# Leaving out the filler matmuls at the three sub-layer boundaries of a two-layer hybrid decoder trunk

## The chip, the cores and the metric

The kernel runs on one core of a Trainium2 chip. The metric is the time of one execution on the device, in microseconds (us); lower is better. A core has TensorE (matrix products, rows PE, with its weight loads PEld), VectorE (DVE), ScalarE (ACT), GpSimd (POOL) and SyncE (SP, which here only issues DMAs). Each engine runs its own instructions in order, and they meet through semaphores.

## The reference

One sequence of 256 tokens of width 1024 goes through two layers. Each layer is a token mixer and a channel mixer, and each of these four sub-layers stands between two root-mean-square norms:

```python
for l in range(DEPTH):                       # DEPTH = 2
    h = rms_norm(x, mix_pre_g[l]) * (1 + sc_m) + sh_m
    y = hybrid_mixer(h, w_in[l], ...)        # conv, stick-breaking attention, gated linear attention, w_o
    x = x + g_m * rms_norm(y, mix_post_g[l])
    h = rms_norm(x, ffn_pre_g[l]) * (1 + sc_f) + sh_f
    y = swiglu(...) if l % 2 == 0 else moe_swiglu(...)   # dense, then top 2 of 8 experts
    x = x + g_f * rms_norm(y, ffn_post_g[l])
```

`rms_norm` divides by the root of the mean square over the 1024 channels. So at a boundary between two sub-layers there is a sum over `y`, an update of `x`, and a second sum over the new `x`, each needed before the next step. The matmuls that the change concerns compute nothing of this.

## The kernel before

Activations lie with channels on the 128 partitions: `x`, `h` and `y` are 8 chunks of 128 channels by 256 tokens. Weights come as units of 1 MB (128 x 2048 floats) in one fixed order (`PLAN`, then the experts). For each unit SP loads `raw`, ACT rounds it to a high part (`write_hi`), DVE subtracts to make a low part (`write_lo`), and PE multiplies high by high, low by high and high by low (`parts`). A unit in `project` is 8 chunks of 6 matmuls of 256 columns.

Each engine's order is written out by hand in its own block. The dense layer and the mixers run unit after unit; the experts run in a loop. Between them lie three boundaries that take the same course: mixer to dense layer in layer 0, dense layer to mixer at the start of layer 1, and mixer to experts in layer 1. One boundary goes:

1. `norm_sums` on PE: matmuls of a matrix of ones (128 x 128) with the squares of `y` give in the bank `M` the sum over channels, on all partitions. This is full fp32, so one matmul leaves two records.
2. `keep_warm(u, 3)` on PE: three filler matmuls of the ones with a constant area of 512 columns, into a bank whose content has been read.
3. ACT `norm`: Ln and Exp give the reciprocal root. DVE `norm_out`: for each of 8 chunks one multiply and one add to `x`. ACT `norm_x` squares `x` two chunks at a time, and after each pair PE adds two matmuls (`norm_sums` again).
4. `keep_warm(u, 2)` on PE: two more fillers.
5. ACT `norm` again; DVE `norm_in` scales each chunk; ACT `shift` adds the bias and rounds; DVE makes the low part and signals `h_split`. PE's first unit (`project` with `ready`) takes up each chunk as it comes. At the third boundary the router's small matmuls come instead, chunk by chunk on `h_ready`.

`keep_warm` issues on PE alone; nothing waits for it and it signals no semaphore. It waits, through `wait_read`, until its bank has been read. No DMA is issued and no other engine's order is touched in it.

Of the kernel before, what the change touches and what calls it, by code (L numbers as in the profile page):

```python
# [30 lines left out]
P = 128  # L31
# [28 lines left out]
PAIRS = D_FF // 256  # L60
# [8 lines left out]
def z_columns():  # L69

    cols = [(CONV, False), (0, False), (CONV + 256, False), (256, False)]
    for part in range(3):
        cols += [(O_SB + 512 * part + 256 * h, part == 2) for h in range(2)]
    for part in range(4):
        cols += [(O_GLA + 512 * part + 256 * h, part == 2) for h in range(2)]
    cols += [(O_GATES + 256 * u, False) for u in range(G_UNITS)]
    return cols
# [98 lines left out]
C_ID, C_ONES, C_LNEG, C_NEG = (A_CONST + P * i for i in range(4))  # L176
# [9 lines left out]
def program(nc, x_t, vecs, c_row, glr_w, a2, router, stream, experts, out_t):  # L186
    with ExitStack() as ctx:
# [19 lines left out]
        bank = [ctx.enter_context(nc.psum_tensor(f"bank{i}", [P, 512], F32)) for i in range(8)]  # L207
# [5 lines left out]
        def area(at, *dims):  # L213
            n = int(np.prod(dims))
            v = ar[:, at:at + n]
            if len(dims) == 2:
                return v.rearrange("p (a b) -> p a b", a=dims[0])
            if len(dims) == 3:
                return v.rearrange("p (a b c) -> p a b c", a=dims[0], b=dims[1])
            return v  # L220
# [31 lines left out]
        ident, ones = area(C_ID, P), area(C_ONES, P)  # L252
# [120 lines left out]
        def mixer_units(layer):  # L373
            return [u for u in W_UNITS if u[1] == layer and u[0] in ("z", "out", "wo")]
# [4 lines left out]
        BANKS = {}  # L379
# [18 lines left out]
        def wait_read(eng, u):  # L398

            for b, before in BANKS[u]:  # L400
                eng.wait_ge(bank_read[b], before + 1)
# [464 lines left out]
        def _(dve):  # L866
# [257 lines left out]
            def moe_lo(step, k, rounds=0):  # L1124
                slot, _, s, w = moe_unit(step, k, rounds)
                dve.wait_ge(hi_written, w + 1)
                dve.tensor_tensor(expert_lo[s], raw[:, slot, :], f32(expert_hi[s]),  # L1127
                                  ALU.subtract).then_inc(raw_taken, 1)
# [210 lines left out]
        def _(pe):  # L1339
# [7 lines left out]
            def norm_sums(first=0, last=4, squares=squares, sums=M):  # L1347

                for q in range(first, last):
                    pe.wait_ge(norm_squares, 4 * norms[0] + q + 1)  # L1350
                    for c in (2 * q, 2 * q + 1):
                        mm = pe.matmul(sums[:, 0:T], ones, squares[:, c, :], start=(c == 0), stop=(c == KC - 1),  # L1352
                                       skip_group_check=True)
                if last == 4:
                    mm.then_inc(norm_sum, 1)
                    norms[0] += 1

            def keep_warm(u, count):

                wait_read(pe, u)  # L1360
                for _ in range(count):
                    pe.matmul(bank[BANKS[u][0][0]][:, :], ones, area(C_ID, 4 * P), start=True, stop=True)

            def begin(u):
                pe.wait_ge(raw_taken, POS[u] + 1)
                for b, before in BANKS[u]:
                    if before:
                        pe.wait_ge(bank_read[b], before)
                return SLOT[u]

            def project(u, hi, lo, ready=None, before=0, chunks=1):


                s = begin(u)
                out = two(bank[BANKS[u][0][0]])
                for k in range(KC):
                    if ready is not None:
                        pe.wait_ge(ready, before + k // chunks + 1)
                    for c in range(2):
                        for n, (w, high) in enumerate(parts(s)):  # L1380
                            mm = pe.matmul(out[:, c, :], w[:, 256 * k + P * c:256 * k + P * c + P],  # L1381
                                           (hi if high else lo)[:, k, :],
                                           start=(k == 0 and n == 0 and c == 0),
                                           stop=(k == KC - 1 and n == 2), skip_group_check=True)
                mm.then_inc(consumed, 1)
# [13 lines left out]
            def project_branch(u, hi, lo):  # L1399

                s = begin(u)
                for c in range(4):
                    out = two(bank[BANKS[u][c // 2][0]])
                    for k in range(4):
                        for n, (w, high) in enumerate(parts(s)):
                            mm = pe.matmul(out[:, c % 2, :], w[:, 512 * k + P * c:512 * k + P * c + P],
                                           (hi if high else lo)[:, k, :],
                                           start=(k == 0 and n == 0), stop=(k == 3 and n == 2))
                mm.then_inc(consumed, 1)
# [134 lines left out]
            def hook(layer, i):  # L1544
                if i == 0:
                    low_rank(layer)
                if 0 <= i - 12 < SB_HEADS:
                    stick_o(layer, i - 12)
                if 0 <= i - 11 < SB_HEADS:
                    stick_sum(layer, i - 11)  # L1550
                if 0 <= i - 10 < SB_HEADS:
                    if i == 10:
                        wait_read(pe, ("z", layer, 7, 0))
                    if i == 12:
                        wait_read(pe, ("z", layer, 9, 0))
                    stick_z(layer, i - 10)
                if i == 19:
                    log_a(layer, 0)
                if i == 20:
                    log_a(layer, 1)  # L1560
                if i == 23:
                    gla_turn(layer)
                if i == 24:
                    gla_states(layer)
                if i == 25:
                    gla_out(layer)
                if i == 26:
                    gla_sums(layer)
                    conv_sums(layer, conv_acc, conv_done, layer + 1, mean_ready)
                if i == 28:  # L1570
                    conv_sums(layer, conv_tmp, cv_squared, layer + 1, var_ready)

            norm_sums()
            for layer in range(DEPTH):
                if layer:
                    norm_sums(1, 4)
                    keep_warm(("gate", 0, PAIRS - 1, 0), 3)
                    norm_sums()
                    keep_warm(("gate", 0, PAIRS - 1, 0), 2)
                for i, u in enumerate(mixer_units(layer)):  # L1580
                    if i == 0:
                        project(u, h_hi, h_lo, h_split, 2 * layer * KC)
                    elif u[0] == "z":
                        (project_tokens if z_columns()[u[2]][1] else project)(u, h_hi, h_lo)
                    elif u[0] == "out":
                        b = u[2]
                        if b == 0:
                            pe.wait_ge(a_split, layer + 1)
                        if b == 2:
                            pe.wait_ge(c_split, layer + 1)  # L1590
                        if i == 32:
                            pe.wait_ge(cv_root, layer + 1)
                        project_branch(u, br_hi[b], br_lo[b])
                    elif u[2] == 0:
                        project(u, h_hi, h_lo, s_split, 4 * layer, 2)
                    else:
                        project(u, h_hi, h_lo)
                    hook(layer, i)
                    if i == 38:
                        norm_sums(0, 2)  # L1600
                norm_sums(2, 4)
                keep_warm(("wo", layer, 2, 0), 3)
                norm_sums()
                keep_warm(("wo", layer, 2, 0), 2)
                if layer == 0:
                    for i, u in enumerate(FFN_UNITS):
                        if u[0] == "down":
                            project_down(u)
                        elif i == 0:
                            project(u, h_hi, h_lo, h_split, KC)  # L1610
                        else:
                            project(u, h_hi, h_lo)
# [3 lines left out]
            for k in range(KC):  # L1616
                pe.wait_ge(h_ready, 3 * KC + k + 1)
                for t in range(2):
                    mm = pe.matmul(Z[0][:, 8 * t:8 * t + 8], hf[:, k, P * t:P * t + P], router_sb[:, k, :],  # L1619
                                   start=(k == 0 and t == 0), stop=(k == KC - 1), skip_group_check=True)  # L1620
# [226 lines left out]
```

## Time and profile before

| | us |
|---|---|
| median of 3 runs | 1854.64 |
| lowest to highest run | 1853.37 to 1854.91 |
| the profiled execution, its own time | 1851.58 |
| its span from first to last instruction | 1849.7 |
| PE busy in the span | 1782.7 |
| mean granted TensorE clock | 0.989 |

Times in rows are microseconds from the first instruction. The granted clock is the share of full speed that TensorE was given: 1.00 is 2.4 GHz, 0.50 is 1.2 GHz. A row of matmuls ends when the last result is out, so the row is longer than the time for which it keeps the next matmul waiting; the distance between two starts in a full queue tells that. "Idle before" in brackets is the time in which the engine stood still, and what released it.

### The profile page before, as it was taken

The page shows a single profiled execution, that of the slowest core. Times are in us where ns is not written, and L with a number is a line of the kernel's source. Part 1 is how long each engine was busy: PE and PEld are TensorE (multiplying, and loading weights), DVE is VectorE, ACT ScalarE, POOL GpSimd, SP SyncE. Part 2 cuts the span into 40 slices and gives each one's busy share as a digit, 9 for nine tenths or more (in the row PEclk, how much of TensorE's full clock was granted, in tenths as well). Part 3 has the DMA queues.
Part 4 walks back from the last instruction along what each step waited for, and adds up shares of the span by engine and source line. Part 5 has one row for each costly group of instructions (what it writes and reads, how often), then busy time and mean ns, then how long its engine had stood idle before and what let it go on. Part 6 is the DMA issues. An engine that isn't in the chain of part 4 may idle for free.

```text
span 1849.7 us, 28685 instructions
## 1 busy us (share of the span) xinstructions
PE 1782.7 (96%) x10843; PEld 1577.2 (85%) x10844; DVE 1533.6 (83%) x1422; ACT 1133.5 (61%) x954; POOL 193.6 (10%) x159
## 2 busy tenths in 40 slices
PE   2999999999999999989999999999999999999997
PEld 2999999899979999978888888888888888888886
DVE  6998866999657667767889898898898988988986
ACT  3444564533354554656777777767777777677774
POOL 0396001000006900000000000000000000000000
PEclk7999999999999999999999999999999999999999
DMA  9865534699735333444999989989999899899992
GB/s 381 356 239 200 175 138 163 229 392 362 260 108 185 135 137 137 160 153 181 364 355 363 373 330 375 366 338 363 353 361 372 330 376 370 335 366 348 361 374 94
DMA packets 72521, 525.30 MB, mean 284 GB/s; under 512 B 8112, under 2 KB 8240, under 8 KB 8704
## 3 DMA queue, kind: packets, MB, share of 16 engines
q1 hardware_dynamic: 72288, 524.03, 74.6%
q8 instruction: 54, 0.88, 0.2%
q0 software_dynamic: 160, 0.23, 0.0%
q14 instruction: 19, 0.16, 0.0%
HBM read 523.17 MB, written 1.05 MB: 283 GB/s over the span
## 4 chain that ended last, share of the span: by engine, by line
PE 55%; DVE 2%; ACT 0%; issue 0%; DVEq 0%; ACTq 0%
PE bank L1654 33%; PE bank L1669 16%; PE bank L1689 2%; PE bank L1679 1%; PE bank L1381 1%; PE bank L1352 1%; PE bank L1709 0%; PE bank L1710 0%; DVE arena L943 0%; DVE arena L947 0%; PE bank L1619 0%; DVE arena L1066 0%; PE bank L1626 0%; DVE w_lo L878 0%; DVE arena L1058 0%
## 5 line engine op out<-in xcount | busy, mean ns | idle before, releaser
L1127 DVE TENSOR_TENSOR w_lo<-raw,w_hi 128x2048 fp32r<-128x2048 f32 x224 | 510.0, 2291 | 82.9 <-ACT w_hi L752 82.9
L752 ACT ACTIVATE w_hi<-raw 128x2048 fp32r<-128x2048 f32 x224 | 428.5, 1916 | 97.0 <-PE bank L1669 70.4
L1381 PE MATMUL bank<-acts,w_hi 128*128 128x256 f32 x2080 | 374.2, 284 | 27.7 <-DVE acts L933 21.1
L1381 PEld LDWEIGHTS bank<-acts,w_hi 128*128 128x128 f32 x2080 | 321.4, 191 | 33.1 <-issue 24.6
L1654 PE MATMUL bank<-acts 128*128 128x512 f32 x1248 | 304.3, 392 | 2.5 <-DVE acts L1127 2.5
L1654 PE MATMUL bank<-w_hi,acts 128*128 128x512 f32 x960 | 297.3, 391 | 0.0
L1381 PE MATMUL bank<-acts,w_lo 128*128 128x256 f32 x1040 | 292.6, 281 | 0.0
L1654 PEld LDWEIGHTS bank<-acts 128*128 128x128 f32 x1248 | 231.3, 188 | 49.3 <-DVE acts L1127 2.9
L1127 DVE TENSOR_TENSOR acts<-raw,acts 128x2048 fp32r<-128x2048 f32 x112 | 256.1, 2287 | 19.9 <-ACT acts L752 19.9
L752 ACT ACTIVATE acts<-raw 128x2048 fp32r<-128x2048 f32 x112 | 215.1, 1921 | 72.2 <-PE bank L1654 69.8
L1669 PE MATMUL bank<-w_hi,acts 128*128 128x512 f32 x832 | 256.1, 389 | 0.0
L878 DVE TENSOR_TENSOR w_lo<-raw,w_hi 128x2048 fp32r<-128x2048 f32 x82 | 190.7, 2325 | 70.3 <-ACT w_hi L542 69.3
L542 ACT ACTIVATE w_hi<-raw 128x2048 fp32r<-128x2048 f32 x82 | 156.7, 1911 | 129.2 <-PE bank L1381 93.5
L1654 PEld LDWEIGHTS bank<-w_hi,acts 128*128 128x128 f32 x960 | 179.0, 188 | 36.3
L1381 PEld LDWEIGHTS bank<-acts,w_lo 128*128 128x128 f32 x1040 | 198.0, 190 | 0.0
L1654 PE MATMUL bank<-w_lo,acts 128*128 128x512 f32 x480 | 186.9, 389 | 0.0
L1669 PEld LDWEIGHTS bank<-w_hi,acts 128*128 128x128 f32 x832 | 156.2, 188 | 32.4
L1669 PE MATMUL bank<-w_lo,acts 128*128 128x512 f32 x416 | 161.9, 389 | 0.0
L891 DVE SCALAR_TENSOR_TENSOR raw<-raw,arena 128x1024 f32<-128x1024 f32 x96 | 116.7, 1252 | 13.1 <-DMA raw<-in_stream 12.1
L1654 PEld LDWEIGHTS bank<-w_lo,acts 128*128 128x128 f32 x480 | 90.1, 188 | 19.0
L489 POOL TENSOR_SCALAR arena<-arena 128x256 f32<-128x256 f32 x60 | 103.4, 1724 | 0.0
L1381 PE MATMUL bank<-acts 128*128 128x256 f32 x816 | 101.3, 284 | 0.0
(234 smaller groups left out, 2120.7 us busy)
## 6 DMA issues: line engine op xcount, KB each, us to landing
raw<-in_experts SPq DMA_DIRECT2D x336, 1024.0 KB, 5.1
raw<-in_stream SPq DMA_DIRECT2D x161, 1024.0 KB, 6.3
arena<-in_x_t SPq DMA_DIRECT2D x1, 1024.0 KB, 11.8
out_t<-arena SPq DMA_DIRECT2D x2, 512.0 KB, 2.6
arena<-in_c_row SPq DMA_DIRECT2D x1, 512.0 KB, 4.7
arena<-in_vecs SPq DMA_DIRECT2D x1, 224.0 KB, 2.5
arena<-in_glr_w POOLq DMA_DIRECT2D x2, 64.0 KB, 4.2
arena<-in_a POOLq DMA_DIRECT2D x2, 32.0 KB, 4.5
```

What stands on the lines that cost most here:

```text
L489: pool.tensor_scalar(product, src, w, None, ALU.mult).then_inc(pool_products, 1)
L542: act.activation(w_hi[SLOT[u]], raw[:, slot, :], ACT.Copy).then_inc(hi_written, 1)
L752: act.activation(expert_hi[s], raw[:, slot, :], ACT.Copy).then_inc(hi_written, 1)
L878: dve.tensor_tensor(w_lo[SLOT[u]], raw[:, POS[u] % RAW, :], f32(w_hi[SLOT[u]]), ALU.subtract).then_inc(raw_taken, 1)
L891: ins = dve.scalar_tensor_tensor(w, w, 1.0, cond[layer], ALU.mult, ALU.mult, accum_out=ar[:, at:at + 1])
L1127: dve.tensor_tensor(expert_lo[s], raw[:, slot, :], f32(expert_hi[s]), ALU.subtract).then_inc(raw_taken, 1)
L1352: mm = pe.matmul(sums[:, 0:T], ones, squares[:, c, :], start=(c == 0), stop=(c == KC - 1), skip_group_check=True)
L1381: mm = pe.matmul(out[:, c, :], w[:, 256 * k + P * c:256 * k + P * c + P], (hi if high else lo)[:, k, :], start=(k == 0 and n == 0 and c == 0),
L1654: mm = pe.matmul(bank[b][:, :], (xe_hi if high else xe_lo)[:, c:c + P], w[:, 512 * kk:512 * kk + 512], start=(half == 0 and kk == 0 and n ...
L1669: mm = pe.matmul(bank[5 + d][:, :], (ae_hi if high else ae_lo)[odd][:, c:c + P], w[:, 1024 * f + 512 * d:1024 * f + 512 * d + 512], start= ...
L1679: mm = pe.transpose(bank[4][:, P * c:P * c + P], act_e[odd][:, P * c:P * c + P], ident)
L1689: mm = pe.matmul((bank[7], bank[2])[half][:, P * c:P * c + P], h_tok[:, at:at + P], sel[:, P * t:P * t + P], start=(t == 0), stop=(t == 1))
```

## The change

The helper `keep_warm` and all its calls are removed. In the code these are two pairs of lines, one at the start of layer 1 and one behind the mixer; the second pair runs in both layers, which makes six calls in an execution, two at each of the three boundaries, and 15 matmuls.

```diff
-            def keep_warm(u, count):
-
-                wait_read(pe, u)
-                for _ in range(count):
-                    pe.matmul(bank[BANKS[u][0][0]][:, :], ones, area(C_ID, 4 * P), start=True, stop=True)
-
@@
                 if layer:
                     norm_sums(1, 4)
-                    keep_warm(("gate", 0, PAIRS - 1, 0), 3)
                     norm_sums()
-                    keep_warm(("gate", 0, PAIRS - 1, 0), 2)
@@
                 norm_sums(2, 4)
-                keep_warm(("wo", layer, 2, 0), 3)
                 norm_sums()
-                keep_warm(("wo", layer, 2, 0), 2)
```

## Rows read from the trace of the kernel before

**Rows 1.** The page, parts 1 and 2: busy time by engine, and granted clock in tenths

```profile
PE 1782.7 (96%) x10843; PEld 1577.2 (85%) x10844; DVE 1533.6 (83%) x1422; ACT 1133.5 (61%) x954; POOL 193.6 (10%) x159
...
PEclk7999999999999999999999999999999999999999
```

**Rows 2.** The page, part 4: the chain that ended last, by engine

```profile
PE 55%; DVE 2%; ACT 0%; issue 0%; DVEq 0%; ACTq 0%
```

**Rows 3.** Waits of PE, 15.3 to 870: who waited for whom, total, times, longest

```profile
PE bank L1381 <- DVE acts L933: 21.1, 3, 18.5
PE bank L1352 <- ACT arena L565: 20.7, 10, 15.3
PE bank L1381 <- DVE acts L1116: 4.4, 2, 2.3
```

**Rows 4.** Waits of PE, 545 to 785

```profile
PE bank L1406 <- DVE arena L1058: 1.2, 2, 0.7
```

**Rows 5.** The fillers by their line: count, shortest, median and longest in ns

```profile
L1362 PE MATMUL bank<-arena x30: 592/592/592, 323.8 to 829.5; 128*128 128x512 f32 x30
```

**Rows 6.** Timeline of PE, first boundary: start, length, line, operation [idle before]

```profile
323.84 2.74 PE L1362 MATMUL bank<-arena 128*128 128x512 f32 x6
327.76 1.13 PE L1352 MATMUL bank<-arena 128*128 128x256 f32 x4 [1.18 <-ACT arena L565]
329.22 1.13 PE L1352 MATMUL bank<-arena 128*128 128x256 f32 x4 [0.33 <-ACT arena L565]
330.68 2.20 PE L1352 MATMUL bank<-arena 128*128 128x256 f32 x8 [0.33 <-ACT arena L565]
332.72 1.88 PE L1362 MATMUL bank<-arena 128*128 128x512 f32 x4
335.90 0.47 PE L1381 MATMUL bank<-acts,w_hi 128*128 128x256 f32 x2 [1.31 <-DVE acts L933]
```

**Rows 7.** Timeline of DVE, first boundary: two low parts of the first unit

```profile
335.33 0.42 DVE L933 TENSOR_TENSOR acts<-arena,acts 128x256 fp32r<-128x256 f32 x1 [0.18 <-ACT arena L576]
...
336.13 0.43 DVE L933 TENSOR_TENSOR acts<-arena,acts 128x256 fp32r<-128x256 f32 x1
```

**Rows 8.** Windows: length, busy PE, PEld, DVE, ACT, POOL (instructions), PEclk, DMA, GB/s

```profile
21.67:24.10 2.43, 0.00 (x0) 0.00 (x0) 2.33 (x5) 0.89 (x2) 0.00 (x0) 1.00 0.98 408
...
40.16:44.60 4.44, 4.44 (x21) 4.44 (x22) 4.07 (x11) 4.44 (x12) 0.00 (x0) 0.50 1.00 411
...
293.50:297.20 3.70, 1.39 (x12) 1.43 (x13) 3.70 (x5) 0.02 (x1) 0.00 (x0) 1.00 0.33 49
297.21:300.60 3.39, 3.39 (x18) 3.39 (x18) 2.75 (x5) 2.51 (x3) 0.00 (x0) 0.50 0.61 256
...
342.20:347.00 4.80, 4.80 (x42) 4.80 (x41) 4.80 (x8) 4.19 (x4) 0.00 (x0) 1.00 0.44 142
...
792.14:795.50 3.36, 3.36 (x18) 3.36 (x17) 3.15 (x6) 2.07 (x3) 0.00 (x0) 0.50 0.66 278
...
856.30:860.00 3.70, 1.26 (x5) 1.05 (x6) 3.70 (x3) 1.90 (x1) 0.00 (x0) 1.00 0.11 18
```

**Rows 9.** Timeline of PE, the kernel's start

```profile
15.30 6.37 PE L1352 MATMUL bank<-arena 128*128 128x256 f32 x16 [15.30 <-ACT arena L565]
...
42.21 0.63 PE L1381 MATMUL bank<-acts,w_hi 128*128 128x256 f32 x2
...
42.85 0.63 PE L1381 MATMUL bank<-acts,w_hi 128*128 128x256 f32 x2
```

**Rows 10.** Timeline of PE, third boundary: the last fillers and the router

```profile
828.23 1.88 PE L1362 MATMUL bank<-arena 128*128 128x512 f32 x4
830.57 4.66 PE L1619 MATMUL bank<-arena 128*128 128x8 f32 x32 [0.45 <-ACT arena L576]
```

**Rows 11.** Windows of the router and what follows, columns as in rows 8

```profile
830.57:833.09 2.52, 2.52 (x23) 2.52 (x23) 2.08 (x6) 2.52 (x7) 0.00 (x0) 1.00 0.83 341
...
833.10:839.90 6.80, 6.71 (x37) 6.34 (x37) 2.64 (x16) 2.51 (x5) 0.00 (x0) 0.50 0.02 6
```

## The prediction

> **What bounds the kernel now.** I read the page first. PE is busy for 1782.7 of 1849.7 us [rows 1], and the chain that ended last runs over PE for 55% of the span and over DVE for 2%; the rest of its shares goes to nothing large [rows 2]. Then I read the waits of PE. Outside the start (18.5 us of the 21.1, and 15.3 us of the 20.7) little stands there: the longest wait that is not at the start or a boundary is one of the two on L1116, 4.4 us together [rows 3]. Behind the first boundary, from 342 to 520, PE has no wait in the profile at all, and from 545 to 785 its longest is 0.7 us, on DVE work that itself follows PE [rows 4]. So a microsecond that PE loses at a boundary isn't given back later, since no other engine is late enough to hide it. What has to be settled is whether PE loses any.
>
> The last view is the granted clock. It stands at nine tenths or more in all slices but the first [rows 1], so the question is how it stays there through the boundaries, and there the fillers are the only thing that works on PE for part of the time.
>
> **What is taken away.** 15 matmuls leave 30 records [rows 5]. At the first boundary six records run from 323.84 and four from 332.72 [rows 6]; the second and third boundary take the same course, with starts that lie within 0.15 us of this pattern. Their direct gain: nothing. After the first group PE still stands idle for 1.18 us until ACT has squared the first pair of `x`, and after the second for 1.31 us until DVE has the first low part [rows 6]. At the third boundary the idle time before the router is 0.45 us [rows 10]. No engine waits for a filler, since they signal nothing, and the wait on the bank is over by then: fillers follow the last sum without a gap [rows 6]. Nothing is added, no DMA is issued and no step is moved. The most that could be gained is the last piece of idle time that a weight load behind a filler might hide, 0.19 us six times or 1.1 us, but PE's start is set by ACT and DVE and I take zero.
>
> **What the idle time then is.** Without fillers PE has nothing to do from 323.84 to 327.76, 3.92 us, and from 332.72 to 335.90, 3.18 us [rows 6]. Between them lie 16 records of sums, which fill 0.88 us of each 1.46 us until the last two pairs. At the third boundary the second gap is 2.34 us, and the router behind it has only 8 columns to each matmul [rows 10].
>
> The trace shows three gaps of such size. At the start PE stopped at 21.67; the clock was 1.00 until 24.1 and then fell, and it came back only after 4.44 us of dense work [rows 8]. In 293.50 to 297.20 PE waited 2.3 us of the L1116 wait and worked for 1.39 us; then the clock was 0.50 for 3.39 us under dense matmuls [rows 8]. The second of the two L1116 waits, 2.1 us by the total less the longest [rows 3], had the same behind it, from 792.14 [rows 8]. Against these stands the stretch 856.30 to 860.00: PE busy for 1.26 us of 3.70, and no fall [rows 8]. The router fell too: busy by the records, with few columns, and from 833.10 half clock for 6.80 us [rows 11]. So gaps of 2.1 to 2.5 us go either way, and both new gaps are longer than any that went well. I expect the first to bring a fall nearly always, the second mostly, and at the third boundary a fall that comes at the router anyhow but may come earlier.
>
> **What a fall costs.** Sums: eight records take from 330.68 to 332.72 less one pause, 0.22 us each at full clock [rows 6]; at the start 16 of them took 6.37 us, 0.40 us each [rows 9]. (The clock column shows full speed there, but the records' length doesn't, and I go by the length.) So a pair of chunks takes 0.88 us warm and 1.6 to 1.7 us cold, against one each 1.46 us from ACT and DVE. A cold stretch of 3.4 us [rows 8] that starts in the gap or with the first pair is nearly made up by the last (+0.2 us). One that starts with the third pair makes both last pairs cold: 3.4 us in place of 2.0, +1.4 us. Where it starts depends on when in the gap the clock falls, which no row fixes for the new kernel; I take the middle, 0.75 us, and keep 0.2 and 1.4 as ends. This delay goes straight to ACT's Ln and on.
>
> First unit: cold, three matmuls start each 0.64 us [rows 9], 1.28 us for a chunk of six. Warm, 42 records take 4.80 us [rows 8], 0.114 us each and 0.69 us a chunk. DVE supplies a chunk each 0.80 us [rows 7]. In 3.4 us cold PE does 2.7 chunks, for which DVE needs 2.1 us: 1.3 us late, and the five chunks left give back 0.11 us each, so +0.75 us. A stretch wholly in dense work costs 3.4 x (1 - 0.114/0.213) = 1.6 us; one that is half over before the first chunk costs 0.2 us or nothing. I take 0.77 us.
>
> Router: 23 records in 2.52 us warm, 0.11 us each; the 9 that follow take 2.1 us of the row of 4.66, some 0.2 us each [rows 10, 11]. Were all 23 cold, that would be 2.3 us; were the stretch moved forward as a whole, the transposes and gathers behind it would get back as much. I take 0.4 us, between -1 and 2.3.
>
> **Sum.** Boundaries one and two: 2 x (0.75 + 0.77) = 3.0 us. Third: 0.75 + 0.4 = 1.15 us. Together +4.2 us. Against the profiled execution of 1851.58 us that is 1855.8 us; the median of the runs shown lies 3.06 us above that execution, and the same sum against it gives 1858.8 us. Bounds: all at the low ends 2 x 0.2 + 0.2 - 1, or about nothing; all at the high ends 2 x (1.4 + 1.6) + 1.4 + 2.3 = 9.7 us.
>
> The Trainium skill, page "TensorE: Matmul & The Clock Gate", section "HAM oscillation — how this bites in real kernels", prices throttled time at its length times (1 - 1.2/2.4), so half. In dense work this trace has nearly that (0.46 of the stretch), but my sum has less because DVE and ACT pace PE there. By the page's rule the six stretches of 3.4 us would cost an estimated 10.2 us in place of 4.2. The same page advises against idle gaps between bursts of matmuls, which is advice against this change.
>
> **The rivals.** Every cold microsecond counts: each of the six gaps brings a fall, each late enough to lie in work that nothing paces. The trace has such a stretch after 297.21 [rows 8], against it stands the pacing of 0.80 us a chunk [rows 7]. Six times 1.6 is 9.5 us, 1864.1 us. The page's rule above would say the same in kind.
>
> Falls that cost little: the clock falls while PE is idle, is back soon, and the lag is made up; 0.2 us in the sums and 0.3 us in the first unit at each boundary, with a little for the router, 2 us, 1856.6 us. For it speaks that at the start the whole fall lay in idle time until 40.16; against it that it took 4.44 us of dense work to come back [rows 8].
>
> The fillers decide nothing: the sums between the gaps are enough work to hold the clock, as after 856.30 [rows 8]. 1854.6 us. Against it: the new gaps are 3.92 and 3.18 us, that one 2.5.
>
> The other side, faster: the clock falls at the first gap of the third boundary, 819 to 823, and is full again where it is half now, over the transposes and gathers of 833.10 to 839.90 [rows 11]. There 6.80 us at half clock hold up to 3.2 us of loss; if the fall after the second L1116 wait (3.4 us, worth 1.6) is missed too by the shift, the gain is 4.8 us. It decides only if the first two boundaries cost under 1 us. 1849.8 us. The router's few columns speak against it, since behind them the clock fell although PE had no idle time.
>
> That the change doesn't do what it says can't be: the records of L1362 are gone with the line.
>
> **How the numbers follow.** The forecast has 0.58, the dear rival 0.14, the cheap one 0.12, no effect 0.12, faster 0.04. A measurement of this kernel tells a difference from none at about 0.2%, 3.7 us, so slower means over 1858.35. The forecast's own spread by the places of the falls is 2.5 to 6 us, and some 0.42 of its 0.58 lies above 3.7 us. Slower: 0.42 + 0.14 = 0.56. Same: 0.16 + 0.12 + 0.12 = 0.40. Faster: 0.04. Range: 1855.0 leaves out the faster case and most of no effect; 1863.0 leaves out the half of the dear rival that lies above it; together 0.2. It takes in the low end, where the lag is made up, and most of the high one.
>
> **What would show it.** The windows of the changed kernel should have a granted clock of 0.50 for 3.4 us or more within each boundary, once or twice. In the timeline the L1352 records of `x` then start 0.43 us apart, and the last ends 0.2 to 1.4 us later behind the last DVE L947 than now; first-unit matmuls start each 0.21 us for a while. The way from the first boundary's last sum of `y` (323.84) to the second unit (342.2, 18.4 us) should grow by about 1.5 us, and no PE wait behind it should shrink. I am wrong if the clock is full at all three, or if it falls and the second unit still starts 18.4 us after; and wrong in a term if the lag is there but PE waits elsewhere get shorter by as much.

## The result

The changed kernel is slower: 1860.04 us median of 7 runs (1856.76 to 1860.43) against 1853.37 us for the kernel before, measured beside it (7 runs, 1852.04 to 1854.91). The ratio is 1.0030 with a 95% interval from 1.0018 to 1.0042, which is 5.6 us. Two repeats of the same kernel, told below, gave 1.0043 and 1.0025. The forecast was 1858.8 us with a range from 1855.0 to 1863.0.

The page of the changed kernel, parts 1 and 2. PE's busy time is 7.4 us less than in [rows 1], since 30 records are gone, and its span 6.1 us more:

```profile
span 1855.8 us, 28625 instructions
...
PE 1775.3 (96%) x10813; PEld 1578.6 (85%) x10814; DVE 1532.9 (83%) x1422; ACT 1133.2 (61%) x954; POOL 191.3 (10%) x159
...
PEclk7999999899999999999999999999999999999999
```

Besides the first slice, the clock row shows one slice under nine tenths, and no more, because stretches at half clock of 3.4 us drown in slices of 46 us. The timeline tells more. This is PE at the first boundary of the changed kernel (columns: start, length, engine, line, operation, idle before); project's matmuls are line 1375 here, the sums 1352 as before:

```profile
323.92 1.98 PE L1352 MATMUL bank<-arena 128*128 128x256 f32 x8
329.65 1.13 PE L1352 MATMUL bank<-arena 128*128 128x256 f32 x4 [3.75 <-ACT arena L565]
331.12 4.44 PE L1352 MATMUL bank<-arena 128*128 128x256 f32 x12 [0.33 <-ACT arena L565]
338.58 0.77 PE L1375 MATMUL bank<-acts,w_hi 128*128 128x256 f32 x2 [3.02 <-DVE acts L933]
339.14 0.41 PE L1375 MATMUL bank<-acts,w_lo 128*128 128x256 f32 x1
...
346.94 5.92 PE L1375 MATMUL bank<-acts 128*128 128x256 f32 x48
```

The idle times of 1.18 and 1.31 us in [rows 6] have become 3.75 and 3.02 us. The three last pairs of sums run through in one row of 4.44 us, where before they had a pause between them. The kernel before has these two rows for the beginning and the end of the same way:

```profile
322.03 1.98 PE L1352 MATMUL bank<-arena 128*128 128x256 f32 x8
...
342.22 5.92 PE L1381 MATMUL bank<-acts 128*128 128x256 f32 x48
```

From the sum of `y` to the second unit it is 20.19 us before and 23.02 us after, 2.8 us more. Windows of the changed kernel (columns as in [rows 8]) show the clock at each boundary:

```profile
323.92:329.65 5.73, 1.98 (x10) 1.25 (x8) 2.66 (x8) 4.40 (x6) 0.00 (x0) 1.00 0.41 163
...
330.94:334.35 3.41, 3.23 (x8) 2.58 (x9) 3.38 (x7) 1.38 (x3) 0.00 (x0) 0.50 0.00 0
334.40:337.70 3.30, 1.15 (x6) 0.67 (x4) 2.01 (x4) 1.52 (x4) 0.00 (x0) 1.00 0.38 89
337.77:344.59 6.82, 6.01 (x28) 6.04 (x29) 5.89 (x15) 6.82 (x16) 0.00 (x0) 0.50 0.27 109
...
536.25:539.10 2.85, 2.85 (x7) 2.30 (x8) 2.85 (x10) 1.25 (x2) 0.00 (x0) 0.50 0.00 0
539.20:545.90 6.70, 3.68 (x22) 3.03 (x21) 5.94 (x11) 4.52 (x11) 0.00 (x0) 1.00 0.43 143
546.00:549.38 3.38, 3.38 (x17) 3.38 (x17) 2.69 (x7) 3.38 (x10) 0.00 (x0) 0.50 0.04 17
...
829.30:832.70 3.40, 3.40 (x9) 2.56 (x9) 3.37 (x10) 1.61 (x3) 0.00 (x0) 0.50 0.00 0
...
839.55:846.30 6.75, 6.66 (x36) 6.29 (x37) 2.65 (x16) 2.39 (x4) 0.00 (x0) 0.50 0.00 0
```

There are two stretches of half clock at each boundary. At the first two boundaries one follows each gap. At the third the first stretch follows the first gap, and the second lies over the router, as it did before [rows 11].

Where the 6.1 us of the two profiles come from, by starts of the same instructions in both timelines. Between the boundaries both traces keep step: from the third unit of the first boundary to the last sum of `y` of the second it is 177.2 us in both, from the third unit of the second boundary to the third boundary likewise 264.2 us, and from the first expert matmul to the end 1006.8 us.

| stretch | before, us | after, us | more |
|---|---|---|---|
| start to last sum of y, first boundary | 322.03 | 323.92 | 1.9 |
| first boundary, to the second unit | 20.19 | 23.02 | 2.8 |
| second boundary, to the second unit | 20.92 | 21.97 | 1.05 |
| third boundary, to the first expert matmul | 25.41 | 25.70 | 0.3 |

The first line isn't of the change: its code is the same, and the changed kernel had by chance a stretch at half clock that the profiled execution of before hadn't. PE is 1.45 us later behind this stretch than ahead of it, against the kernel before; another 0.3 us was there at the first matmul. This row of the changed kernel has 18 matmuls where a full clock has about 29 (42 in 4.80 us, [rows 8]):

```profile
105.70:109.00 3.30, 3.30 (x18) 3.30 (x17) 3.26 (x4) 0.00 (x0) 3.22 (x3) 0.50 0.99 392
```

### The profile page after: what moved, and what is told of

Read it like the earlier page. It is cut to its first block, busy times and chain, and to the rows that moved or that the text cites. A ratio compares the mean times of both kernels' runs of the same rounds, so it can differ in the third digit from the quotient of the medians.

```text
span 1855.8 us, 28625 instructions
## 1 busy us (share of the span) xinstructions
PE 1775.3 (96%) x10813; PEld 1578.6 (85%) x10814; DVE 1532.9 (83%) x1422; ACT 1133.2 (61%) x954; POOL 191.3 (10%) x159
## 3 DMA queue, kind: packets, MB, share of 16 engines
HBM read 523.17 MB, written 1.05 MB: 282 GB/s over the span
## 4 chain that ended last, share of the span: by engine, by line
PE 55%; DVE 2%; ACT 1%; issue 0%; DVEq 0%; ACTq 0%
PE bank L1644 32%; PE bank L1659 16%; PE bank L1679 2%; PE bank L1669 1%; PE bank L1375 1%; PE bank L1352 1%; PE bank L1699 0%; PE bank L1700 0%; DVE arena L943 0%; PE bank L1609 0%; DVE arena L1066 0%; PE bank L1616 0%; DVE arena L947 0%; DVE arena L1285 0%; DVE w_lo L878 0%
```

## The experiments

Each is the kernel before with one edit, timed beside it.

**One gap at a time.** First the fillers of the first gap are left out and those of the second stay, then the other way round.

```diff
-                    keep_warm(("gate", 0, PAIRS - 1, 0), 3)
-                keep_warm(("wo", layer, 2, 0), 3)
```

> Only the three fillers of the first gap of each boundary are left out; the two of the second gap stay. Theory A (the fillers keep the clock, each gap has its own price): half clock at each boundary behind the first gap, the sums of x up to 1.4 us later, but no second stretch in the first unit unless the first runs on; per boundary +0.3 to +1.4 us, together +2.5 us (1 to 4). Rival B (a fall of the clock costs nothing since DVE and ACT pace the boundary): falls are seen but the time is that of before, within 1 us. Rival C (one gap alone does no harm, it needs both): no falls at the boundaries, time as before.

```diff
-                    keep_warm(("gate", 0, PAIRS - 1, 0), 2)
-                keep_warm(("wo", layer, 2, 0), 2)
```

> Only the two fillers of the second gap of each boundary are left out; the three of the first gap stay. Theory A: the sums of x are at full speed and end as in the kernel before, 10.5 us after the first record of the last sum of y; the first unit starts at half clock in most executions, and the unit behind it starts 0.2 to 1.6 us later; together with the router +2 us (0.5 to 4). With the run without the first group the two add up to about what the whole change costs, 5 to 6 us. Rival B: time of before within 1 us. Rival C: no falls.

Measured: 1.0019 (1.0010 to 1.0028) without the first group, 1.0017 (1.0008 to 1.0026) without the second; 3.5 and 3.2 us. Windows of the two profiles, first of the kernel without the first group, at the three boundaries:

```profile
329.90:333.30 3.40, 3.40 (x9) 2.30 (x8) 3.37 (x9) 1.89 (x3) 0.00 (x0) 0.50 0.00 0
534.75:538.10 3.35, 3.15 (x8) 2.49 (x9) 3.31 (x7) 1.41 (x3) 0.00 (x0) 0.50 0.00 0
824.85:831.60 6.75, 5.40 (x13) 4.32 (x14) 6.71 (x14) 2.88 (x5) 0.00 (x0) 0.50 0.01 2
```

and of the kernel without the second group, the gap and the first unit of the first boundary, and the first unit of the second:

```profile
334.50:337.30 2.80, 0.00 (x0) 0.00 (x0) 2.10 (x6) 2.22 (x6) 0.00 (x0) 1.00 0.48 117
337.45:340.90 3.45, 3.45 (x17) 3.45 (x18) 3.45 (x10) 3.45 (x10) 0.00 (x0) 0.51 0.50 207
542.25:545.70 3.45, 3.45 (x19) 3.45 (x18) 3.45 (x9) 3.45 (x10) 0.00 (x0) 0.51 0.42 176
```

Each gap alone brings its own fall, and each kernel costs time of its own. Theories B (a fall is free here) and C (both gaps are needed) are out. The sum of the two, 6.7 us, is in line with 5.6 us within their intervals.

The cost is shown by the timings, not by these two profiles. By starts of the same matmuls, the three boundaries together add 0.9 us in the first profile and 1.8 us in the second, while the spans are 5.4 and 6.3 us over that of before. Most of the rest lies in stretches at half clock where the code is that of before. Three of them in the kernel without the first group:

```profile
104.65:107.95 3.30, 3.30 (x18) 3.30 (x17) 3.27 (x5) 0.00 (x0) 3.22 (x4) 0.50 1.04 412
862.40:865.70 3.30, 3.30 (x9) 2.53 (x8) 3.30 (x3) 0.00 (x0) 0.00 (x0) 0.50 0.88 330
1838.60:1841.90 3.30, 3.30 (x16) 3.21 (x15) 2.51 (x4) 1.84 (x3) 0.00 (x0) 0.50 0.00 0
```

The profile of before has none of the three and is among its shortest executions (span 1849.7 us; the 27 beside the last repeat have 1849.5 to 1853.3, mean 1851.6). The profile of the kernel with more fillers at the start, told below, has all three. So the span of one profile can't be set against that of another, and what a boundary costs is taken from its own starts or from many executions.

**Busy but not streaming.** The fillers keep their time and lose their columns:

```diff
-                for _ in range(count):
-                    pe.matmul(bank[BANKS[u][0][0]][:, :], ones, area(C_ID, 4 * P), start=True, stop=True)
+                for _ in range(4 * count):
+                    pe.matmul(bank[BANKS[u][0][0]][:, 0:8], ones, area(C_ID, 8), start=True, stop=True)
```

> Each filler of 512 columns is replaced by four of 8 columns, so that PE is occupied for about as long (24 records of 0.11 us in the first gap, 16 in the second) but streams almost nothing. Theory A, in the form that streamed work holds the clock, as the router suggests: the clock falls at the boundaries as in the changed kernel, and the time is that of the changed kernel, 4 to 7 us above before. Rival D (an engine that isn't idle holds the clock): no fall, the time of before.

Measured: 1.0028 (1.0017 to 1.0040), 5.2 us. The timeline of PE and two windows of its profile:

```profile
323.20 1.98 PE L1352 MATMUL bank<-arena 128*128 128x256 f32 x8
325.02 2.74 PE L1362 MATMUL bank<-arena 128*128 128x8 f32 x24
328.93 1.13 PE L1352 MATMUL bank<-arena 128*128 128x256 f32 x4 [1.17 <-ACT arena L565]
330.40 4.32 PE L1352 MATMUL bank<-arena 128*128 128x256 f32 x12 [0.33 <-ACT arena L565]
```

```profile
330.00:333.40 3.40, 3.07 (x8) 2.45 (x8) 3.37 (x8) 1.61 (x3) 0.00 (x0) 0.50 0.02 5
...
541.65:548.40 6.75, 6.04 (x28) 6.07 (x29) 5.26 (x13) 6.75 (x17) 0.00 (x0) 0.50 0.23 97
```

This is the sharpest of the runs. The filler row is as long as in [rows 6], 2.74 us, and PE's idle time behind it is 1.17 us against 1.18. By busy time the two kernels can't be told apart there, and yet the clock falls and the time is that of the kernel without fillers. What differs is the columns: with fillers of 512 the clock held in this gap, with fillers of 8 it fell, at equal idle time. It fell behind the first gap of all three boundaries and behind the second gap of the second. Behind the second gap of the first boundary it held in this profile, with fillers of 8 columns too:

```profile
337.74:344.07 6.33, 6.33 (x49) 6.10 (x49) 5.58 (x13) 6.33 (x14) 0.00 (x0) 1.00 0.18 75
```

Rival D is out, and with it the thought that the removed instructions had another use, for instance as a pause.

**The changed kernel again.** Twice more, without an edit against it.

> The changed kernel once more, for a second profile. Theory A with places that differ from execution to execution: each boundary costs between 0.2 and 3 us against before, not the same as in the first profile (2.8, 1.05 and 0.3 us); the part ahead of the first boundary, which in the first profile held 1.9 us more than before, does not hold it again or does so by chance, since its code is the same. Rival E (the removal also changes what runs ahead of the first boundary): 1.9 us there again, with a fall at 105.7.

> The changed kernel a third time, for the size of its cost and for a third profile. Seven and six executions so far gave ratios of 1.0030 and 1.0043 to before; I expect 1.0035 (1.0025 to 1.0045), with spans that scatter over some 8 us and are longer the lower the mean granted clock is, by nearly half a microsecond for each microsecond at half clock.

Measured: 1.0043 (1.0028 to 1.0058) from 6 runs and 1.0025 (1.0016 to 1.0034) from 11. All 24 runs of the changed kernel together have a median of 1858.1 and a mean of 1858.9 us; the runs of before beside the third had a median of 1853.5. In the two new profiles the first boundary costs 2.6 and 2.7 us, the second 1.0 twice, the third 0.3 twice. The last sum of `y` at the first boundary starts at 322.08 and 322.19, as in the kernel before, so rival E (the change acts ahead of the first boundary) is out; and the kernel with the fillers left out at the third boundary alone, told below, has the stretch near 105 too.

The spans scatter from 1852.9 to 1863.0 us, where the 27 runs of before beside the last repeat scatter over 3.6 us, and they follow the mean granted clock. Four of the 24, the two shortest and the two longest:

```
span 1852.9 us, clock 0.986
span 1853.2 us, clock 0.986
span 1862.2 us, clock 0.980
span 1863.0 us, clock 0.977
```

From 0.986 to 0.977 the time at half clock grows by about 2 x 0.009 x 1856, 33 us, and the span by about 10 us. A straight line through all 24 gives 0.30 us for each microsecond at half clock, and not nearly half, as I had expected. All three profiles lie among the shorter executions, 1853.8 to 1855.8 us of span against a mean of 1856.9.

**One boundary at a time.** The fillers are left out at one boundary and stay at the two others: at the first and at the third by a condition on the layer,

```diff
-                keep_warm(("wo", layer, 2, 0), 3)
+                if layer:
+                    keep_warm(("wo", layer, 2, 0), 3)
```

(`if layer == 0` for the third, and the same for the second group), and at the second by taking out the pair with `"gate"`.

> The fillers are left out at the first boundary alone (layer 0, mixer to dense layer). Theory A: the way from the boundary's last sum of y to the second unit grows from 20.2 us to between 20.6 and 23; in the two profiles of the changed kernel it grew by 2.8 and 2.6 us, so the time is +2.4 us (1 to 3). My prediction had 1.52 us for this boundary. Rival F (each boundary costs the same on average, a third of 5.6 us or so): +1.9 us; F and A differ only together with the run of the third boundary alone.

> The fillers are left out at the third boundary alone (layer 1, mixer to experts). Theory A as the two profiles of the changed kernel have it: only +0.3 us, since the clock falls at the router in the kernel before too. My prediction had 1.15 us, and rival F says +1.9 us. If it is near 2 us, the two profiles were no fair sample of the executions.

> The fillers are left out at the second boundary alone (start of layer 1). By difference of the mean spans so far (all three 6.2, the first alone 2.7, the third alone 1.0) it is +2.5 us over before. If the boundaries add up it lies between 1.5 and 3.5 us; if it is at the 1.0 us that its two profiles show, the three don't add up, or the profiles are low draws. My prediction had 1.52 us.

| left out at | ratio, 95% interval | mean span over that of before, us | in its profile, us |
|---|---|---|---|
| first | 1.0012 (1.0003 to 1.0021) | 2.7 | 2.7 |
| second | 1.0017 (1.0008 to 1.0026) | 3.3 | 2.9 |
| third | 1.0003 (0.9994 to 1.0012) | 1.0 | 0.2 |

The three ratios add up to 0.32%, the whole change has 0.25 to 0.43%. The third boundary can't be told from nothing, while the first two can. So rival F, the same cost at each, doesn't fit well, though its interval for the third ends at 2.2 us. The second cost 2.9 us in this profile and 1.0 us in the three of the changed kernel; the windows of this run show why, with 6.75 us at half clock over the first unit in place of 3.38:

```profile
533.55:536.90 3.35, 3.35 (x8) 2.71 (x9) 3.32 (x6) 1.26 (x2) 0.00 (x0) 0.50 0.00 0
540.35:547.10 6.75, 6.03 (x28) 6.06 (x29) 5.27 (x13) 6.75 (x17) 0.00 (x0) 0.50 0.25 104
```

The third boundary has no fixed price either, since the stretch over the router varies with its code unchanged. In the kernel with the fillers left out at the first boundary alone, it lasted 3.4 us and not 6.8:

```profile
821.22 1.98 PE L1352 MATMUL bank<-arena 128*128 128x256 f32 x8
...
845.01 0.72 PE L1656 MATMUL bank<-w_hi,acts 128*128 128x512 f32 x2
```

```profile
837.80:841.15 3.35, 3.25 (x21) 2.88 (x21) 2.58 (x16) 1.19 (x2) 0.00 (x0) 0.50 0.00 0
841.20:861.60 20.40, 17.90 (x105) 15.51 (x104) 14.95 (x38) 13.16 (x14) 0.00 (x0) 1.00 0.14 53
861.70:865.05 3.35, 3.35 (x10) 2.61 (x9) 3.35 (x3) 0.00 (x0) 0.00 (x0) 0.50 0.87 313
```

From the last sum of `y` to the first expert matmul it is 23.79 us here, 1.6 us less than the 25.41 of before, and the fall from 861.70 takes 1.5 us of that back. The profiles of two more kernels with fillers at this boundary show the same (the one without them at the second boundary, and the one with more at the start). So the 0.2 to 0.3 us in the profiles holds against one profile of before, and the mean over the executions, 1.0 us, is no better known than its interval.

**One filler fewer in each group.**

```diff
-                keep_warm(("wo", layer, 2, 0), 3)
+                keep_warm(("wo", layer, 2, 0), 2)
```

(and 2 to 1 in the second gap, and both at the other boundary)

> One filler fewer in each group: two in the first gap and one in the second. PE is then idle for about 2.2 us in the first and 2.3 us in the second gap, as long as in the waits on L1116, behind which the clock fell in some profiles and not in others. Theory A: falls at some boundaries in some executions, a cost between those of before and of the changed kernel, +1.5 us (0 to 3.5). If gaps of this length are harmless at a boundary, the time is that of before.

Measured: 1.0019 (1.0010 to 1.0028), 3.5 us, the upper end of what I expected. PE is idle for 2.04 us in the first gap now (1.93 us at the second boundary), and the clock falls:

```profile
329.24 1.13 PE L1352 MATMUL bank<-arena 128*128 128x256 f32 x4 [2.04 <-ACT arena L565]
```

```profile
330.95:334.30 3.35, 3.35 (x9) 2.54 (x9) 3.32 (x6) 1.26 (x2) 0.00 (x0) 0.50 0.00 0
535.75:539.10 3.35, 3.35 (x9) 2.40 (x8) 3.32 (x6) 1.26 (x2) 0.00 (x0) 0.50 0.00 0
```

In this profile the sums end 0.9 us later than before at each of the first two boundaries, and behind the second gap (2.17 us idle at both) the clock holds. At the third boundary it holds behind both gaps. So in this profile it is the first group that is too small with two fillers; of the second group with one filler the run shows no harm.

**More fillers.** Does the kernel gain where the clock is still low? The start has 20.5 us at half clock, and behind the two waits on L1116 it fell as well.

```diff
                     if i == 0:
+                        for _ in range(0 if layer else 21):
+                            pe.matmul(bank[BANKS[u][0][0]][:, :], ones, area(C_ID, 4 * P), start=True, stop=True)
                         project(u, h_hi, h_lo, h_split, 2 * layer * KC)
```

and in the kernel with both also

```diff
                     elif u[2] == 0:
+                        begin(u)
+                        for _ in range(2):
+                            pe.matmul(bank[BANKS[u][0][0]][:, :], ones, area(C_ID, 4 * P), start=True, stop=True)
                         project(u, h_hi, h_lo, s_split, 4 * layer, 2)
```

> The kernel before with 21 more fillers ahead of the first unit, from 21.7 to about 39.6 us, where PE waits for its first input for 18.5 us and the clock is at half until 44.6. Theory A: the clock is full by 40.2 (granted clock 1.00 there), the first unit takes 6.3 us in place of 7.8, and the time is 1.3 us less than before (0.5 to 2). Rival B (a fall costs nothing where DVE sets the pace): the same time as before. A cost of its own, if the fillers run over the first input: up to 1 us more.

> The 21 fillers at the start and two more in each of the two waits on L1116, 2.3 and 2.1 us, ahead of the output projection. Theory A: no fall behind these waits in any profile; in the kernel before both were there in its one profile and one on average in the others, each worth 1.5 us; with the start -2.5 us against before (-1 to -4). Rival B: no change.

Measured: 1.0001 (0.9992 to 1.0010) with the start alone, 0.9996 (0.9987 to 1.0005) with both. Neither differs from before. Windows and two timeline rows of the kernel with the fillers at the start:

```profile
24.20:40.16 15.96, 15.34 (x36) 6.46 (x34) 11.61 (x21) 4.84 (x5) 0.00 (x0) 1.00 1.01 420
40.54:44.60 4.06, 4.06 (x31) 3.94 (x32) 3.85 (x10) 4.06 (x11) 0.00 (x0) 1.00 1.01 422
```

```profile
96.67 0.50 PE L1394 MATMUL bank<-w_hi,acts 128*128 128x256 f32 x2 [0.52 <-DVE w_lo L878]
...
104.74 0.50 PE L1381 MATMUL bank<-acts,w_hi 128*128 128x256 f32 x2 [2.14 <-DVE w_lo L878]
```

and the one of the kernel before at the same place:

```profile
104.37 0.50 PE L1381 MATMUL bank<-acts,w_hi 128*128 128x256 f32 x2 [1.55 <-DVE w_lo L878]
```

The clock is full, and the first unit takes 6.41 us in place of 7.82: 1.4 us are won. Then PE waits for DVE, 0.52 and 2.14 us in place of 1.55, and from the first unit to this point it is 64.20 us in the one kernel and 64.21 in the other. All of it is given back. Here rival B is right: DVE is the engine that comes last (from 44 to 105 it is busy for 60.1 of 61.0 us in both kernels), and the fall of the clock at the start costs nothing.

In the kernel with both, the clock was full behind the L1116 waits too, and the time didn't follow by an amount that could be measured. The traces say why. These are the rows of PE from the first L1116 wait on, first in the kernel before, where the clock fell at 297.2, then in the changed kernel, where it didn't:

```profile
295.81 0.48 PE L1381 MATMUL bank<-acts,w_hi 128*128 128x256 f32 x2 [2.32 <-DVE acts L1116]
...
303.51 0.50 PE L1381 MATMUL bank<-acts,w_hi 128*128 128x256 f32 x2 [0.32 <-DVE w_lo L878]
```

```profile
297.69 0.47 PE L1375 MATMUL bank<-acts,w_hi 128*128 128x256 f32 x2 [2.32 <-DVE acts L1116]
301.39 0.51 PE L1375 MATMUL bank<-acts,w_hi 128*128 128x256 f32 x2 [0.64 <-DVE acts L1116]
305.41 0.50 PE L1375 MATMUL bank<-acts,w_hi 128*128 128x256 f32 x2 [1.01 <-DVE w_lo L878]
```

```profile
297.69:305.41 7.72, 6.07 (x49) 5.68 (x49) 6.51 (x9) 5.43 (x5) 0.00 (x0) 1.00 0.39 136
```

It is 7.70 us with half clock and 7.72 us without: what PE loses, it would otherwise have waited for DVE. The second L1116 wait is alike, 7.70 us with the fall (before, from 791.14) and 7.70 us with full clock (first repeat of the changed kernel, from 794.83). So both falls behind these waits in the profile of before were free. I expected 1.3 us less with the start alone and 2.5 us less with both; for both, the interval allows 2.4 us less to 0.9 us more. Theory A stands for the boundaries and fails as a rule for every stretch at half clock.

## Why the prediction was right

The sign, the cause and the size within its range were right; the forecast of 1858.8 us stood against 1860.04 in the first measurement and 1858.1 as the median of all 24 runs. That it came so close is in part luck. As a difference it was 4.2 us and 5.6 us were measured, and it was added to a median of before (1854.64, three runs) that was 1.3 us above that of the seven runs beside the changed kernel. In the profiles the terms missed one by one and made each other up: 2.8 us at the first boundary in place of 1.5, 1.05 at the second in place of 1.5, 0.3 at the third in place of 1.15.

*The fillers hide no work and cost none.* Right. The first pair of sums starts 5.73 us behind the last sum of `y` in both kernels (322.03 to 327.76, 323.92 to 329.65), and no kernel with fewer fillers was faster than before.

*The first gap always falls, the second mostly.* Right in the three profiles of the changed kernel: both at the first two boundaries, and at the third the first, with the router behind it as before. That 8-column work doesn't hold the clock I had used for the router only; the narrow fillers showed it behind the first gap of each boundary.

*The price in the sums, 0.75 us between 0.2 and 1.4.* In the three profiles 0.6 to 0.8 us at the first boundary, 0.0 at the second, 0.3 at the third. At the second the clock was at half from the first pair on (536.25) and full again from 539.20, so that the last pairs made the lag up entirely: the low end should have been nothing.

*The price in the first unit, 0.77 us.* This is the term that was mis-sized. It was 2.0 us at the first boundary and 1.0 us at the second. I had put one stretch of 3.4 us there, from the stretches behind the L1116 waits [rows 8]. But at the first boundary it lasted 6.8 us, and 6.0 us of it under the unit's matmuls: 6.0 / 1.28 is 4.7 chunks, which DVE delivers in 3.8 us, and the lag of 2.2 us less three chunks at 0.11 makes 1.9. A row that could have warned me was in the list: at the start, where PE begins from idle as it does here, the clock stayed at half for 4.44 us of work [rows 8], more than 3.4.

*The router, 0.4 us.* Too dear in the profiles: from the last sum of `x` to the first expert matmul nothing was added, since the stretch at half clock there is as long as in the profile of before and lies over the same work. The third boundary had 1.15 us in the sum and measured 1.0 us by mean spans, 0.2 to 0.3 us in the profiles.

*The sum.* In the three profiles the boundaries cost 4.2, 3.9 and 4.0 us, the forecast's number; over the executions the mean was 5.4 us. That in others the stretches fall in dearer places fits the second boundary, which cost 1.0 us in three profiles and 2.9 in another kernel's, but no profile of a long execution of the changed kernel shows it. The prediction had no term for that but its range, up to 9.7 us.

*A stretch wholly in dense work, 1.6 us.* Near, in two places: the stretch from 105.70 cost 1.45 us and the one from 861.70 1.5 us. But I had taken the ones behind the L1116 waits for such stretches, and those cost nothing: DVE paced PE there too. So the dear rival's example [rows 8] was none, and of the 4.8 us that the faster case could have won, 1.6 weren't there to be won.

*What would show it.* I wanted 1.5 us more from the last sum of `y` to the second unit at the first boundary, and the way grew by 2.8 us. (The 323.84 that I gave as its start is the first filler's; the sum starts at 322.03.)

*Nothing is given back later.* Right: the profile has no wait of PE between the first boundary and 520 in either kernel, and the way from boundary to boundary is the same to 0.1 us. The run with more fillers shows the opposite case 240 us earlier in the same kernel.

*The rivals.* "Every cold microsecond counts" was the Trainium skill's rule in kind (page "TensorE: Matmul & The Clock Gate", section "HAM oscillation — how this bites in real kernels": half of the throttled time). In the first profile the boundaries have 20.5 us of half clock more than before, by the rule an estimated 10.2 us; measured were 4.2. Over executions of the changed kernel the share was about 0.3, and at the start and behind the L1116 waits 0. "No effect" is out by the interval. The faster case did not come in the three profiles: the fall over the router moved with the router. Kernels with fillers there had the shorter fall that this case hoped for, and lost 1.5 us again behind it, near 861.

What stays open: the profiles are few against the executions that were timed, so how often the dearer places are hit is known only from the spread of spans and clocks. So the 1.4 us or so between the mean cost and that of the profiles is not placed.

## What to carry to other kernels

When an engine waits between bursts, look first at who is late behind the wait. If PE is the only engine with no slack afterwards, as behind these boundaries, the time by which it comes late stays in the total, and a filler that fits into the gap is free; if another engine sets the pace, as at the start and behind the L1116 waits, it buys nothing. Don't judge a filler by the busy time it adds: here 8 columns added as much as 512, and the clock fell. Read the granted clock behind the gap, and read it in more than one profile, since the same boundary cost 1.0 us in one and 2.9 in another.

## What was not expected of the hardware

Behind a row of matmuls that keeps PE busy for 2.74 us with 8 columns each the clock fell just as behind idle time (24 records, idle time 1.17 us against 1.18 with wide fillers, granted clock 0.50 from 330.0). Idle times of 2.04 and 1.93 us were followed by a fall (the run with one filler fewer), while in the same profile two of 2.17 us were not. Stretches at half clock behind a 2.3 us wait cost nothing (7.70 against 7.72 us), while one of the same length under dense work cost 1.45 us. Where PE began from idle on work that DVE paced, half clock lasted 6.8 us at the first boundary in all three profiles of the changed kernel, twice the 3.4 us under dense work. The first sums of the kernel run at 0.40 us a record beside a granted clock that the profile gives as 1.00 [rows 9]; the length of the instruction is the surer sign.
